# A decoder layer on one core: gate and up of 20 of 22 column tiles by seven half-block products, and the down weights' sums by adding DMAs

## The reference

```
mix = hybrid_mixer(x, ...)
h   = layer_norm(ALPHA * x + mix, ln1_g, ln1_b)
g   = silu(h @ w_gate) * (h @ w_up)       # w_gate, w_up: 1024 x 2816
out = layer_norm(ALPHA * h + g @ w_down, ln2_g, ln2_b)
```

## Time and profile before

| | us |
|---|---|
| median of 3 runs | 704.86 |
| the profiled execution | 705.2 |
| its span, first to last instruction | 703.4 |
| TensorE busy | 689.1 (98%) |
| VectorE busy | 431.3 (61%) |
| ScalarE busy | 336.7 (48%) |
| GpSimd busy | 141.3 (20%) |

### The profile page before, as it was taken

How to read it: one execution, slowest core, us unless ns; L and a number is a source line. 1 busy time by engine, 2 the same in 40 slices (tenths; PEclk the granted TensorE clock), 3 DMA queues, 4 the chain that set the end, 5 groups by cost and what they waited for, 6 DMA issues and landing times.

```text
span 703.4 us, 9442 instructions
## 1 busy us (share of the span) xinstructions
PE 689.1 (98%) x3380; PEld 577.2 (82%) x3380; DVE 431.3 (61%) x739; ACT 336.7 (48%) x624; POOL 141.3 (20%) x129
## 2 busy tenths in 40 slices
PE   8999999999999999999999999999999999999985
PEld 6987888888888888888998888888888888888873
DVE  5569997767876236647923442233334337989897
ACT  5678787467766344333223222222222225677741
POOL 2110000000001000000236664355533415100000
PEclk9999999999999999999999999999999999999998
DMA  8221112211114522361357556654466433676643
GB/s 320 78 92 61 61 62 89 90 61 61 61 61 133 226 90 91 114 215 61 102 188 248 210 209 217 230 197 154 161 233 209 149 106 103 184 221 211 187 126 135
DMA packets 34723, 102.09 MB, mean 145 GB/s; under 512 B 3584, under 2 KB 3712, under 8 KB 34688
## 3 DMA queue, kind: packets, MB, share of 16 engines
q1 hardware_dynamic: 27504, 74.36, 31.8%
q0 software_dynamic: 7184, 27.27, 11.7%
HBM read 87.99 MB, written 13.63 MB: 144 GB/s over the span
## 4 chain that ended last, share of the span: by engine, by line
PE 88%; DVE 5%; ACT 3%; issue 1%; DMA 1%; POOL 0%; SPq 0%; DVEq 0%
PE ps L1376 22%; PE ps L1378 22%; PE ps L1377 22%; PE ps L1709 4%; PE ps L1711 4%; PE ps L1710 4%; PE ps L1458 2%; PE ps L1444 2%; PE ps L1414 1%; ACT rope L593 1%; DVE sl L857 1%; PE ps L1409 1%; DMA x_raw<-in_xT 1%; PE ps L1419 1%; DVE sl L849 1%
## 5 line engine op out<-in xcount | busy, mean ns | idle before, releaser
L857 DVE TENSOR_TENSOR sl<-raw,sh 128x512 fp32r<-128x512 f32 (+1 forms) x113 | 111.8, 989 | 77.2 <-ACT sh L807 77.2
L1376 PE MATMUL ps<-hTh,sh 128*128 128x512 f32 x320 | 124.5, 389 | 0.0
L1377 PE MATMUL ps<-hTh,sl 128*128 128x512 f32 x320 | 124.5, 389 | 0.0
L1378 PE MATMUL ps<-hTl,sh 128*128 128x512 f32 x320 | 124.5, 389 | 0.0
L807 ACT ACTIVATE sh<-raw 128x1024 fp32r<-128x1024 f32 x36 | 38.2, 1062 | 146.3 <-PE ps L1378 127.6
L849 DVE TENSOR_TENSOR sl<-raw,sh 128x1024 fp32r<-128x1024 f32 x50 | 61.8, 1236 | 54.7 <-ACT sh L577 54.5
L1376 PE MATMUL ps<-xh,sh 128*128 128x512 f32 x208 | 83.7, 403 | 0.0
L1378 PE MATMUL ps<-xl,sh 128*128 128x512 f32 x208 | 81.3, 391 | 0.0
L1377 PE MATMUL ps<-xh,sl 128*128 128x512 f32 x208 | 81.1, 390 | 0.0
L577 ACT ACTIVATE sh<-raw 128x1024 fp32r<-128x1024 f32 x50 | 52.8, 1058 | 42.8 <-PE ps L1378 36.4
L1378 PEld LDWEIGHTS ps<-hTl,sh 128*128 128x128 f32 x320 | 60.1, 188 | 12.6
(11 more groups left out here) (217 smaller groups left out, 1297.3 us busy)
## 6 DMA issues: line engine op xcount, KB each, us to landing
raw<-in_slabs SPq DMA_DIRECT2D x86, 512.0 KB, 3.3
stage<-in_wdn POOLq DMA_DIRECT2D x11, 1024.0 KB, 9.1
tw<-tsum POOLq DMA_DIRECT2D x11, 1024.0 KB, 5.7
raw<-tw SPq DMA_DIRECT2D x44, 256.0 KB, 2.8
raw<-in_wdn SPq DMA_DIRECT2D x33, 256.0 KB, 2.9
x_raw<-in_xT SPq DMA_DIRECT2D x8, 256.0 KB, 6.1
res<-in_x POOLq DMA_DIRECT2D x1, 2048.0 KB, 8.9
late_raw<-in_slabs SPq DMA_DIRECT2D x4, 512.0 KB, 4.2
```

The source lines that it names most:

```text
L857: return dve.tensor_tensor(dst, src, hi.bitcast(F32), ALU.subtract)
L1376: pe.matmul(dst, lh, rh, start=start, stop=False)
L1377: pe.matmul(dst, ll, rh, start=False, stop=False)
L1378: return pe.matmul(dst, lh, rl, start=False, stop=stop)
```

## The change

Two of the 22 column tiles, those of `LATE`, stay as they are. For each of the other 20, gate and up are taken together as a 2 x 2 block matrix (gate and up by upper and lower half of the 1024 input rows) times the 2 x 2 blocks of the hidden states (upper and lower half of the rows, left and right 256 tokens). Seven products of half blocks, each 4 chunks x 3 matmuls that move 256 tokens, replace the eight. The blocks' sums:

- Three sums of the hidden states, and a fourth in place of one block, are made once, by VectorE from a float32 copy `hT_f` that ScalarE writes (`keep_h`, `v_sums`), and split into `vt` (and over a part of `hTh`, `hTl`).
- Four sums of the weights are made per column by VectorE in place in the raw buffer (`s1_s3`, `s2`, `s4`).
- The products' sums are formed in PSUM where two follow each other in one bank, with ScalarE copying intermediate values out (`keep_x`, `keep_z`), and VectorE making up's right half, gate, and the two halves of the hidden block.

A column's raw weights, five blocks of 256 KB (one block is held twice), come in one load of 1.25 MB into one of two buffers. The hidden sums (D5, S6, S7) move from GpSimd to VectorE. The sums T1 to T4 are made by GpSimd's DMAs within DRAM: a copy of the pair's weights to `tw`, then three transfers that add to what is there, each after the one before has landed; seven pairs after slab 5, the other four after x has landed. TensorE's order in a column and its waits are below.

```diff
+P1, P5, P6, P2, P7, P3, P4 = range(1, 8)
+SEVEN = 7
+X_BANK = (2, 4)
+YZ_BANK = (3, 5)
+HALF = SEQ // 2
+V5, V6, V7 = range(3)
+RAW_A11, RAW_S1, RAW_S3, RAW_A12, RAW_A22, RAW_BLOCKS = range(6)
+W_SLOT = {P1: 0, P5: 1, P6: 2, P7: 3, P2: 4, P3: 5, P4: 6}
+SPLITS = ((RAW_A11, 0, 2, P5), (RAW_S1, 2, 1, P6), (RAW_S3, 3, 2, P7), (RAW_A12, 5, 2, P4))
+ITEM_SLOT = (7, 0, 1, 2, 4, 3, 5, 6)
...
+            for k in range(N_SEVEN):
+                if k == 0:
+                    sp.wait_ge(lo_ready, N_FF)
+                elif k == 1:
+                    sp.wait_ge(hT_done, TB)
+                else:
+                    sp.wait_ge(split_lo, 4 * (k - 1))
+                sp.dma_start(raw_f[k % 2][:, :, :], gu[k][:, 0:RAW_BLOCKS, :]).then_inc(column_landed[k % 2], 16)
...
+            def t_sums(i):
+                pool.dma_start(flat(tw[i]), flat(wdn[i])).then_inc(t_copied, 16)
+                pool.wait_ge(t_copied, 16 * (i + 1))
+                pool.dma_start(flat(tw[i, T1:T3 + 1]), flat(wdn[i, W12:W22 + 1]), accum_op=ALU.add,
+                               max_dma_last_dim=4096).then_inc(t_first, 16)
+                pool.wait_ge(t_first, 16 * (i + 1))
+                pool.dma_start(flat(tw[i, T2:T2 + 1]), flat(tw[i, T1:T1 + 1]), accum_op=ALU.add,
+                               max_dma_last_dim=4096).then_inc(t_second, 16)
+                pool.wait_ge(t_second, 16 * (i + 1))
+                pool.dma_start(flat(tw[i, T4:T4 + 1]), flat(tw[i, T2:T2 + 1]), accum_op=ALU.add,
+                               max_dma_last_dim=4096).then_inc(t_made, 16)
+            T_FIRST = 7
+            pool.wait_ge(slab_done, N_QF)
+            for i in range(T_FIRST):
+                t_sums(i)
...
+            for i in range(T_FIRST, PAIRS):
+                t_sums(i)
...
-            load_stage(0)
-            weight_sums(0)
-            for i in range(PAIRS):
-                if i + 1 < PAIRS:
-                    weight_sums(i + 1)
-                hidden_sums(i)
...
+            def column_hi(k, u):
+                first, at_slot, blocks, user = SPLITS[u]
+                if u == 0:
+                    act.wait_ge(s3w_made, k + 1)
+                elif u == 1:
+                    act.wait_ge(s2_made, k + 1)
+                elif u == 3:
+                    act.wait_ge(s4_made, k + 1)
+                if k:
+                    act.wait_ge(product_done, SEVEN * (k - 1) + user)
+                elif u == 0:
+                    act.wait_ge(slab_done, N_FF)
+                act.activation(sh[:, 512 * at_slot:512 * (at_slot + blocks)],
+                               raw_f[k % 2][:, first:first + blocks, :].rearrange("p b n -> p (b n)"), ACT.Copy)\
+                    .then_inc(split_hi, 1)
+            def keep_x(k, q):
+                if q == 0:
+                    act.wait_ge(ff_done, k + 1)
+                act.wait_ge(product_done, SEVEN * k + (P6 if q else P1))
+                act.activation(sg[:, k % 2, q * HALF:(q + 1) * HALF], ps[:, X_BANK[k % 2], 0:HALF], ACT.Copy)\
+                    .then_inc(x_kept, 1)
+            def keep_z(k):
+                act.wait_ge(product_done, SEVEN * k + P5)
+                if k >= 2:
+                    act.wait_ge(up2_made, k - 1)
+                act.activation(zt[:, k % 2, :], ps[:, YZ_BANK[k % 2], HALF:SEQ], ACT.Copy).then_inc(z_kept, 1)
...
+            for k in range(N_SEVEN - 1):
+                column_hi(k, 3)
+                keep_x(k, 0)
+                keep_z(k)
+                column_hi(k + 1, 0)
+                keep_x(k, 1)
+                column_hi(k + 1, 1)
+                column_hi(k + 1, 2)
+                silu(k + FF_PLAIN)
...
+            def column_lo(k, u):
+                first, at_slot, blocks, _ = SPLITS[u]
+                dve.wait_ge(split_hi, 4 * k + u + 1)
+                cols = slice(512 * at_slot, 512 * (at_slot + blocks))
+                low(sl[:, cols], raw_f[k % 2][:, first:first + blocks, :].rearrange("p b n -> p (b n)"), sh[:, cols])\
+                    .then_inc(split_lo, 1)
+            def s1_s3(k):
+                r = raw_f[k % 2]
+                dve.wait_ge(column_landed[k % 2], 16 * (k // 2 + 1))
+                dve.tensor_tensor(r[:, RAW_S1, :], r[:, RAW_S1, :], r[:, RAW_S3, :], ALU.add).then_inc(s1_made, 1)
+                dve.wait_ge(s1_made, k + 1)
+                dve.tensor_tensor(r[:, RAW_S3, :], r[:, RAW_A11, :], r[:, RAW_S3, :], ALU.add).then_inc(s3w_made, 1)
+            def s2(k):
+                r = raw_f[k % 2]
+                dve.wait_ge(split_lo, 4 * k + 1)
+                dve.tensor_tensor(r[:, RAW_S1, :], r[:, RAW_S1, :], r[:, RAW_A11, :], ALU.add).then_inc(s2_made, 1)
+            def s4(k):
+                r = raw_f[k % 2]
+                dve.wait_ge(split_lo, 4 * k + 3)
+                dve.wait_ge(s2_made, k + 1)
+                dve.tensor_tensor(r[:, RAW_A12, :], r[:, RAW_S1, :], r[:, RAW_A12, :], ALU.add).then_inc(s4_made, 1)
+            def up_right(k):
+                dve.wait_ge(product_done, SEVEN * k + P7)
+                dve.wait_ge(z_kept, k + 1)
+                if k >= 2:
+                    dve.wait_ge(ff_done, k + 1)
+                dve.tensor_tensor(up2[:, k % 2, :], zt[:, k % 2, :], ps[:, X_BANK[k % 2], 0:HALF], ALU.add)\
+                    .then_inc(up2_made, 1)
+            def gate(k):
+                dve.wait_ge(product_done, SEVEN * k + P3)
+                dve.wait_ge(x_kept, 2 * k + 2)
+                dve.tensor_tensor(sg[:, k % 2, :], sg[:, k % 2, :], ps[:, YZ_BANK[k % 2], :], ALU.add)\
+                    .then_inc(gate_made, 1)
...
+                    dve.wait_ge(up2_made, k + 1)
+                    dve.scalar_tensor_tensor(out=h[:, HALF:SEQ], in0=up2[:, k % 2, :], scalar=-1.0,
+                                             in1=sg[:, k % 2, HALF:SEQ], op0=ALU.mult, op1=ALU.mult)
+                    dve.wait_ge(product_done, SEVEN * k + P4)
+                    dve.scalar_tensor_tensor(out=h[:, 0:HALF], in0=ps[:, X_BANK[k % 2], 0:HALF], scalar=-1.0,
+                                             in1=sg[:, k % 2, 0:HALF], op0=ALU.mult, op1=ALU.mult).then_inc(ff_done, 1)
...
+            s1_s3(0)
+            column_lo(0, 0)
+            v_sums(0)
+            v_sums(1)
+            v_sums(2)
+            v_low(1, hT_f[:, 0:4, 0:HALF], vt[:, V5, 0, :, :], vt[:, V5, 1, :, :])
+            v_sums(3)
+            s2(0)
+            v_low(2, hT_f[:, 4:8, HALF:SEQ], vt[:, V6, 0, :, :], vt[:, V6, 1, :, :])
+            hidden(0)
+            column_lo(0, 1)
+            v_low(3, hT_f[:, 0:4, HALF:SEQ], vt[:, V7, 0, :, :], vt[:, V7, 1, :, :])
+            column_lo(0, 2)
+            s4(0)
+            hidden(1)
+            v_low(4, hT_f[:, 4:8, 0:HALF], hTh[:, 0:4, HALF:SEQ], hTl[:, 0:4, HALF:SEQ])
+            for k in range(N_SEVEN - 1):
+                if k:
+                    hidden(k + FF_PLAIN - 1)
+                s1_s3(k + 1)
+                column_lo(k, 3)
+                column_lo(k + 1, 0)
+                s2(k + 1)
+                if k % 2 == 0:
+                    hidden_sums(k // 2)
+                column_lo(k + 1, 1)
+                up_right(k)
+                column_lo(k + 1, 2)
+                gate(k)
+                s4(k + 1)
...
+            def product(p, bank, cols, bh, bl, start):
+                for c in range(KC // 2):
+                    w = slice(W_SLOT[p] * 512 + c * P, W_SLOT[p] * 512 + (c + 1) * P)
+                    dst = ps[:, bank, cols]
+                    pe.matmul(dst, sh[:, w], bh[:, c, :], start=start and c == 0, stop=False, skip_group_check=True)
+                    pe.matmul(dst, sl[:, w], bh[:, c, :], start=False, stop=False, skip_group_check=True)
+                    last = pe.matmul(dst, sh[:, w], bl[:, c, :], start=False, stop=c == KC // 2 - 1,
+                                     skip_group_check=True)
+                last.then_inc(product_done, 1)
+            def column(i, r, first):
+                x, yz = X_BANK[r], YZ_BANK[r]
+                pe.wait_ge(split_lo, i * 8 + (4 * r + 1))
+                pe.wait_ge(ff_done, i * 2 + (r + 1))
+                product(P1, x, left, hTh[:, upper, left], hTl[:, upper, left], True)
+                if first:
+                    pe.wait_ge(v_lo_made, 1)
+                product(P5, yz, right, vt[:, V5, 0, :, :], vt[:, V5, 1, :, :], True)
+                pe.wait_ge(split_lo, i * 8 + (4 * r + 2))
+                pe.wait_ge(x_kept, i * 4 + (2 * r + 1))
+                if first:
+                    pe.wait_ge(v_lo_made, 2)
+                product(P6, x, left, vt[:, V6, 0, :, :], vt[:, V6, 1, :, :], False)
+                pe.wait_ge(split_lo, i * 8 + (4 * r + 3))
+                pe.wait_ge(z_kept, i * 2 + (r + 1))
+                product(P2, yz, left, hTh[:, lower, left], hTl[:, lower, left], False)
+                pe.wait_ge(x_kept, i * 4 + (2 * r + 2))
+                if first:
+                    pe.wait_ge(v_lo_made, 3)
```

(18 more changed lines are left out.)

274 lines of the change are left out of this document (157 added, 117 removed).

## The result

The changed kernel takes 693.37 us (median of four runs, 692.93 to 693.59), the kernel before 704.9 us beside it (704.56 to 705.35). The ratio is 0.983, 95% interval [0.982, 0.985]: 11.5 us less. The profiled run took 693.18 us with a span of 691.5.

The account below looks back on a forecast made before the run. TensorE was taken as the only bound in the feed-forward loop. From the profiled 705.2 us, -16.0 + 3.4 + 1.0 + 1.0 gave 694.6, or 694.3 against the runs' median, which is 0.3 lower; range 691 to 698 (0.58).

Parts of the forecast that it names:

- The matmuls: Feed-forward loop: a column falls from 10.88 to 10.08 us with 256-column steps of 120.0 ns; 16.0 us less over 20.
- The first column: First column: VectorE's work laid end to end delays P6 by 2.3 us and P4 by 0.9; 3.4 us in all.
- Even columns: Columns with hidden sums: the hand-over chain makes P4 0.1 us late in nine columns; 1 us, bounds 0 and 12.
- The end of the loop: Start of the down product: GpSimd's eleven sums slow VectorE's items to 2.03 us; 1.0 us charged, bounds 0 and 2.
- The loads and the DRAM sums: Column loads of 5.7 us and DRAM sums of 20 us per pair before LayerNorm 1 all hide; nothing charged.
- A: Rival in the column loop: longer hand-overs let VectorE set the column's length; 700 us, 705 and more at worst; chance 0.14.
- B: Rival before LayerNorm 1: dependent DRAM transfers don't fit, deciding from 24 us per pair; 714 to 757 us; chance 0.08.
- B2: Rival in the DRAM sums: few of 16 DMA engines share a transfer, 33 to 46 us per pair; 785 and more; 0.05.
- C: Rival in the column loop: the 1.25 MB load lands late, at 8 us instead of 5.7; 705 us; chance 0.05.
- D: Rival for the whole change: everything hides, first column and end too; 689 us; chance 0.10.

Follow-up runs that it names:

- Experiment 1: The kernel before with each feed-forward slab's matmuls in two halves of 256 tokens, eight products of half blocks per column: 718.63 us.
- experiments 2 and 3: Changed kernel, first column only: 2 reordered ScalarE's queue, 694.45 us; 3 also moved VectorE's up's right half before the next column's low part, 693.79 us.
- experiment 4: Changed kernel with one more VectorE reduction of 512 elements (0.60 us) in every column: 701.15 us.
- experiment 7: Changed kernel with GpSimd's eleven sums at the end cut from 256 to 8 columns, output not the layer's: 691.85 us.
- both cuts: Changed kernel with GpSimd's eleven end sums cut to 8 of 256 columns and LayerNorm 2's two loads to 64 of 1024: 691.55 us.
- experiment 6: Changed kernel with six pairs of DRAM sums first instead of seven, leaving five before LayerNorm 1: 696.78 us.

## Why the prediction was right

694.3 us was forecast and 693.4 measured. In the profiled runs loop and end part together changed by -13.05 + 1.2 = -11.85 us, where the sum had -10.6.

**The matmuls, -16.0.** Right. The loop before was 20 x 10.88 = 217.6 and the steps after are 201.6. Experiment 1 shows the step's price in another kernel (12.78 us for 12.8).

**The first column, +3.4.** Measured 1.84 before P6 and 0.81 before P4 for my 2.3 and 0.9, with 0.1 us in the step behind each some 2.9. Place and order are right: VectorE laid end to end. P6 started at 373.49 where I had 374.1. I named ScalarE's split as what stands ahead; experiments 2 and 3 say that the split was only first in line, and VectorE's backlog, which I had also laid out, the cause.

**Even columns, +1.0.** This is the term that was off: nothing was measured. The chain of seven hand-overs came out at 8.46 us where I had 8.55. The error is the 0.2 us for P4's weight load, which I took off the due time as if the load had to wait for its own semaphore ahead of the matmul's start. In experiment 4 P4 starts 0.06 us after up's right half ends, and the real price of a wait is the lateness plus 0.1 us in the next step. So P4 was in time by 0.12 us (0.18 less the 0.06), not late by 0.1. That agrees with experiment 4, where 0.13 us of the 0.6 were absorbed. The mechanism is right, but that the loop ran free hung on a tenth of a us, which no row of the kernel before could settle; the prediction's own bounds for this term went to 12 us.

**The end of the loop, +1.0.** The end part is 1.2 us longer, and experiment 7 shortens it by 0.54 us and the total by 1.5. The mechanism and the place (a pause of 0.51 us at 587.69, smaller ones around it) are the prediction's. What I hadn't seen is that LayerNorm 2's loads take VectorE's lead as well: with the sums cut it still falls to nothing, and only both cuts bring back the end part of the kernel before. Nor had I seen that a lead which is missing at 650 us lengthens the last wait; in the changed kernel this did not happen, in most of its variants it did, by 1 us or more.

**The loads and the DRAM sums, 0.** 1.25 MB land in 5.4 and 5.6 us for my 5.7. A pair's chain took 16.7 us in the emptiest stretch (52.46 to 69.11), 17 to 21 in the others, and 25 for the last one; I had 20, and the last four took 20.3 on average. The pieces stand in this row of the DMA view (the 1 MB copy, us to landing) and in the two `tw` rows above:

```profile
tw<-in_wdn POOLq DMA_DIRECT2D x11, 6.3
```

So 6.3, 6.2 and 4.5 us for my 9, 6 and 4. All of it hides, and the last transfer is issued 12.4 us before the right half.

**The rivals.** A (VectorE sets the column) did not come, but is 0.12 us away: experiment 4 made it. B did not come; experiment 6 shows its door, one pair further. B2 is refuted: four engines would need an estimated 12.7 us for the 1 MB copy at the rate of the earlier trace rows, and it took 6.3. The Trainium skill, "DMA: Bandwidth & Descriptors" (section on why a DMA increments its semaphore by 16), applies its rule to the access pattern as the instruction carries it, and names an exception for some copies issued by GpSimd. The source's four blocks needn't be what the instruction carried; which of the two it was no run here shows. C is out with 5.6 us. D, all hidden, missed what the first column and the end cost, 4 us.

## What to carry to other kernels

Price a matmul by the distance between starts at the size that the change uses: seven products save an eighth of the columns, and here the smaller step took 11 of those 27 us. Where work moves to an engine that then is 90% busy, follow one column's chain of hand-overs against its due time: 0.12 us of margin held through the loop, and 0.6 us more on VectorE in every column cost 7.8 of the 11.5 us. At a joint between two loops ask how much lead the feeding engine has left; two loads that cost nothing measurable with three items ready cost 3 us with none. And two causes that eat the same lead don't add up: cutting one of them alone can look worthless.

## What the runs showed of the hardware

Adding DMAs from DRAM to DRAM took about one and a half times as long as plain loads: 512 KB in 6.2 us and 256 KB in 4.5, against 4.5 for a slab's 512 KB beside them and 2.9 for an item's 256 KB. The slabs' loads had taken 3.3 us without them. No time was lost by it: the loop starts at 368.77 us in both kernels.

TensorE's clock fell after some waits. The matmuls behind the wait before the last product, in the changed kernel:

```profile
666.12 0.62 PE L1963 MATMUL ps<-sh,ah 128*128 128x512 f32 x1 [1.87 <-DVE res L1465]
666.53 0.63 PE L1964 MATMUL ps<-sh,al 128*128 128x512 f32 x1
666.96 0.63 PE L1965 MATMUL ps<-sl,ah 128*128 128x512 f32 x1
```

Steps of 0.43 us instead of 0.227, for eight matmuls: the granted clock is 0.57 of full speed from 666 to 670 us, most of it at 1.2 GHz. The length of the wait doesn't tell whether this happens. The clock stayed at 1.00 behind an idle time of 1.88 us in the kernel before, 1.87 with both cuts, 2.16 with the sums cut, and 3.56 in experiment 1:

```profile
691.59 0.47 PE L1710 MATMUL ps<-sh,ah 128*128 128x512 f32 x1 [3.56 <-DVE res L1297]
...
691.00:697.00 6.00, 5.41 (x24) 4.54 (x25) 5.96 (x14) 2.39 (x6) 0.00 (x0) 1.00 0.31 76
```

It fell behind 1.87 us in the changed kernel and behind 2.87 to 4.19 in the nine others, for 6 to 14 matmuls, whose steps were 1.4 to 2.9 us too long in all. Little of that reached the total: from the end of that wait to the last matmul it takes 16.98 to 17.06 us in the four kernels that kept the clock and 16.91 to 17.63 in the ten that didn't, because VectorE sets the next wait too, and it came out shorter (0.59 us in the changed kernel, 1.03 in the kernel before).
